# Modulation rows of a two-layer diffusion transformer: two parts first by stationary weights, the other rows in 32-column strips beside other stages

## The chip, the cores and the metric

The kernel runs on one core of one Trainium2 chip. The metric is the device time of one execution in microseconds (us).

## The reference

Two layers (D = 1024) over 256 context tokens and 1024 latent tokens, all in 32-bit floats. In each layer the conditions c and c_ctx give a modulation vector of six parts of 1024 values:

```python
def adaln(cond, w, b):
    mod = jax.nn.silu(cond) @ w + b        # w: (1024, 6144)
    return jnp.split(mod[:, None, :], 6, axis=-1)
...
def modulate(x, shift, scale):
    return x * (1 + scale) + shift
```

Parts 0 and 1 are shift and scale ahead of the token mixer, part 2 the gate on its result, parts 3 and 4 shift and scale ahead of the experts, part 5 the gate on their sum. The token mixer projects the modulated tokens, runs a windowed attention (8 heads) and a latent attention (8 heads, dense), merges the two by sigmoid gates and projects the result. After a layer norm a router chooses for each of 16 experts 128 latent tokens (and in layer 0 also 32 context tokens) by top-k. The experts' SwiGLU results, times part 5, are added into the stream, and a second layer norm ends the layer.

## The kernel before

One instruction stream is written by hand for each engine: TensorE (PE) for all products and transposes, VectorE (DVE) and ScalarE (ACT) for what reads PSUM, GpSimd (POOL) for copies and indirect DMAs, and SyncE (SP) for nearly all loads and stores. A stream waits on counters (`wait_ge`). On SP a DMA is issued when all before it in the stream have been.

The stages of a layer, in order:

1. *Modulation rows of layer 0* (`ada_products(0)`). SP loads w_ada in 12 chunks of 512 columns (2 MB each, `ada_chunk`), and between them the projection weights. For a chunk PE multiplies eight times with the two condition vectors as the stationary side (128x2) and 512 columns of weights moving, and adds the bias with a ninth product of one row (L594). ACT copies the 2x512 result out, POOL stores it to `mod_rows` in DRAM, SP loads all 96 rows of 128 back, PE transposes them, ACT copies them to `modT`, and DVE adds 1 to the scales.
2. *Projections*, one tile of 128 tokens after another (ten tiles). The first waits for all projection weights (`wp_in`).
3. *Attention*, four latent blocks of two tiles, eight head pairs each; layer 0 has a ctx block of eight head pairs before. A head pair n has three parts: A and B (two heads of the latent attention) and W (the window heads). For each part PE computes the scores, DVE finds the maximum, ACT computes the exponentials, PE transposes them in three groups (ci = 0, 1, 2: four, four and two blocks of 128) into PSUM banks 6 and 7 in turn, and ACT or DVE copies each group to `PT` (`copy_chunks`, `copy_chunk`). A bank is free for the next group when its copy is done (`pt_a` counts the copies of ACT, `pt_d` those of DVE, `free_bank` waits).
4. *Merge* (`merge_block`): eight blocks f of 128 output channels, each over three token chunks (256, 512, 512). Per chunk PE multiplies the outputs of both attentions (4 + 4 products) and the gate inputs (8 + 8). SP loads the block's 1.5 MB of weights (`weights`) into one of two buffers, in a loop over pairs of blocks.
5. *Output projection and layer norm* (`y_step`), one tile after another. PE computes 16 products of 512 columns, the router product of two tiles before (`router`, 16 columns), and eight transposes of the tile before; DVE reads y first (`y_used`), then norms.
6. *Choice of tokens*: softmax, transposes of the affinities, top-k on DVE, `select`. In layer 0, PE computes the 12 chunks of layer 1's rows here, eight before `select` and four after it, with the first two chunks loaded during stage 5.
7. *Experts*: 16 experts, weights through a ring of 12 slots of 1 MB. POOL gathers tokens and scatters the results.

`mms` (L575 before, L621 after) and `tr` (L579, L625) issue most products and transposes, so their lines stand for many places. SP's loads all have line L354.

## Time and profile before

| | us |
|---|---|
| median of three runs | 4645.54 (4643.63 to 4647.64) |
| the profiled execution | 4643.44 |
| its span, first to last instruction | 4641.9 |
| PE busy in the span | 4342.7 (94%) |
| DVE, ACT, POOL busy | 1358.6, 1022.7, 211.5 |
| attention of layer 0 with its context block, 457 to 951: PE busy | 473.14 of 494 |
| merge of layer 0, 951 to 1368: PE busy | 412.72 of 417 |
| output tiles of layer 0, 1368 to 1540: PE busy | 164.73 of 172 |
| one head pair in the steady attention (transposes at 804.53, then 818.44) | 13.91 |
| one merge block (SP at 1003.21, then 1054.78) | 51.57 |
| one output tile in the loop (y at 1451.87, then 1469.04) | 17.17 |

The profile is one execution. Its PE products of 32-bit floats stand there as two records each, so a product of 512 columns is two records. "Idle before" a row is the time in which that engine stood still right before it, with the operation that released it. The granted clock is a share of 2.4 GHz: 1.00 or 0.50.

### The profile page before, as it was taken

How to read it: one execution, taken by the hardware profiler on the slowest of the kernel's cores; microseconds unless marked ns; L12 is line 12 of the kernel's file. 1: busy time of each engine (PE TensorE's matmuls, PEld its weight loads, DVE VectorE, ACT ScalarE, POOL GpSimd, SP SyncE). 2: the span in 40 equal slices, each digit the busy share in tenths (PEclk: the TensorE clock that was granted, in tenths of full speed). 3: DMA queues.
4: the chain of work that ended last, by engine and by line, in shares of the span. 5: the costliest groups of instructions: out<-in, count | busy, mean ns of one | idle time of the engine just before them, and what ended most of it. 6: DMA issues, size and time to landing. Idle time of an engine off the chain costs nothing.

```text
span 4641.9 us, 64584 instructions
## 1 busy us (share of the span) xinstructions
PE 4342.7 (94%) x24906; PEld 3015.4 (65%) x24906; DVE 1358.6 (29%) x3311; ACT 1022.7 (22%) x2363; POOL 211.5 (5%) x252
## 2 busy tenths in 40 slices
PE   8998999999999889999999798999999984999995
PEld 1454666655545359999998455666644444999995
DVE  0232655611114711111110444556410145111113
ACT  0222655510002111111110323555400120000001
POOL 0000000000000010000000000000000000000001
PEclk9999999999999999999999899999999996999998
DMA  8112000111223478888877221001112333999994
GB/s 297 57 47 64 19 15 14 35 59 30 67 77 117 163 248 260 263 264 263 250 239 235 96 77 51 15 14 41 37 41 72 120 121 127 312 315 315 309 315 165
DMA packets 577960, 653.08 MB, mean 141 GB/s; under 512 B 36792, under 2 KB 511368, under 8 KB 577808
## 3 DMA queue, kind: packets, MB, share of 16 engines
q1 hardware_dynamic: 562736, 605.71, 40.8%
q0 software_dynamic: 15072, 45.20, 3.9%
q8 instruction: 114, 1.87, 0.2%
q14 instruction: 38, 0.31, 0.0%
HBM read 579.97 MB, written 70.88 MB: 140 GB/s over the span
## 4 chain that ended last, share of the span: by engine, by line
PE 60%; issue 22%; DVE 5%; DMA 1%; ACT 1%; DVEq 0%; POOL 0%; POOLq 0%; SPq 0%; ACTq 0%
PE PS L575 38%; PE PS L865 6%; PE PS L579 5%; PE PS L728 4%; PE PS L794 2%; PE PS L787 1%; PE PS L971 1%; PE PS L706 1%; DVE arena L1534 1%; DVE arena L1536 1%; DVE arena L1229 1%; DVE arena L1540 1%; DVE arena L1383 1%; PE PS L800 0%; PE PS L714 0%
## 5 line engine op out<-in xcount | busy, mean ns | idle before, releaser
L575 PE MATMUL PS<-arena 128*128 128x160 f32 (+6 forms) x14144 | 2947.9, 370 | 31.8 <-DMA arena<-in_b_ada 13.0
L575 PEld LDWEIGHTS PS<-arena 128*128 128x128 f32 (+1 forms) x14144 | 2085.9, 189 | 874.2 <-issue 755.3
L1229 DVE TENSOR_TENSOR arena<-arena,PS 128x160 f32<-128x160 f32 (+3 forms) x336 | 125.1, 382 | 1608.8 <-ACT arena L1209 938.0
L579 PEld LDWEIGHTS PS<-arena 128*128 128x128 f32 (+1 forms) x3078 | 368.9, 142 | 332.2 <-issue 211.6
L579 PE MATMUL PS<-arena 128*128 128x128 f32 (+1 forms) x3078 | 472.0, 280 | 80.1 <-DVE arena L1229 45.7
L728 PE MATMUL PS<-arena 96*128 96x512 f32 (+1 forms) x800 | 363.7, 537 | 33.6 <-DMA arena<-q_window 18.2
L1209 ACT ACTIVATE arena<-PS 128x160 f32<-128x160 f32 (+1 forms) x256 | 74.5, 291 | 1370.3 <-PE PS L575 1370.3
L865 PE MATMUL PS<-arena 128*128 128x512 f32 x576 | 259.5, 605 | 18.2 <-DVE arena L1229 9.9
L1372 DVE TENSOR_REDUCE arena<-PS 128x1 f32<-128x512 f32 (+1 forms) x384 | 229.9, 600 | 117.9 <-PE PS L728 95.7
L1092 ACT ACTIVATE arena<-PS 128x256 f32<-128x256 f32 (+1 forms) x408 | 198.5, 487 | 238.5 <-PE PS L579 234.3
L865 PEld LDWEIGHTS PS<-arena 128*128 128x128 f32 x576 | 108.6, 193 | 149.7 <-issue 125.2
L1229 DVE TENSOR_TENSOR arena<-PS,arena 128x640 f32<-128x640 f32 (+6 forms) x330 | 113.6, 385 | 284.5 <-ACT arena L1100 145.3
L1082 ACT ACTIVATE arena<-PS,arena 128x1280 f32<-128x1280 f32 (+1 forms) x144 | 177.5, 1233 | 83.7 <-DVE arena L1374 67.1
L1229 DVE TENSOR_TENSOR arena<-arena 128x2 f32<-128x2 f32 (+6 forms) x332 | 165.9, 500 | 67.9 <-ACT arena L1145 23.5
L1131 ACT ACTIVATE arena<-PS 128x512 f32<-128x512 f32 (+1 forms) x40 | 22.2, 554 | 703.5 <-PE PS L575 703.5
L1590 DVE SCALAR_TENSOR_TENSOR arena<-PS,arena 128x512 f32<-128x512 f32 x64 | 48.1, 751 | 378.6 <-PE PS L575 378.6
L728 PEld LDWEIGHTS PS<-arena 96*128 96x128 f32 x800 | 123.3, 194 | 50.4 <-issue 44.5
L794 PE MATMUL PS<-arena 128*64 128x128 f32 x2624 | 155.5, 273 | 0.1
L794 PEld LDWEIGHTS PS<-arena 128*64 128x64 f32 x2624 | 145.7, 137 | 0.4 <-ACT arena L1092 0.4
L1400 DVE CUSTOM_DVE_ANT_0 arena<-PS,arena 128x640 f32<-128x640 f32 (+1 forms) x144 | 111.6, 775 | 96.3 <-PE PS L579 70.7
L1383 DVE COPY arena<-PS 128x512 f32<-128x512 f32 x192 | 131.1, 683 | 3.8 <-PE PS L579 3.8
L1074 ACT ACTIVATE arena<-arena 128x640 f32<-128x640 f32 (+1 forms) x144 | 114.2, 793 | 62.0 <-DVE arena L1404 54.9
(151 smaller groups left out, 1791.0 us busy)
## 6 DMA issues: line engine op xcount, KB each, us to landing
arena<-in_w_exp_gate SPq DMA_DIRECT2D x128, 1024.0 KB, 6.9
arena<-in_w_exp_up SPq DMA_DIRECT2D x128, 1024.0 KB, 9.0
arena<-in_w_exp_down SPq DMA_DIRECT2D x128, 1024.0 KB, 7.7
arena<-in_w_ada SPq DMA_DIRECT2D x24, 2048.0 KB
arena<-in_w_in SPq DMA_DIRECT2D x32, 512.0 KB, 5.4
h_transposed<-arena SPq DMA_DIRECT2D x20, 512.0 KB, 4.2
x_mid<-arena SPq DMA_DIRECT2D x18, 512.0 KB, 2.7
moe_sum<-arena SPq DMA_DIRECT2D x18, 512.0 KB, 2.9
```

The lines of the kernel that those rows point to most:

```text
L575: m = pe.matmul(o, lt, rh, start=start and i == 0, stop=stop and i == n - 1)
L579: return pe.transpose(o, i, ident)
L728: pe.matmul(PS[:, b + i, 0:cn], qMt[0:MQ, u, h, :], kT[0:MQ, h, i * 512:i * 512 + cn], start=True, stop=True).then_inc(s["sM"], 1)
L794: pe.matmul(PS[half(g), 6, P:2 * P], V[:, kt, half(2 * c + g)], PT[:, place("AB"[g], n, kt), :], start=kt == 0, stop=kt == nm - 1)
L865: m = pe.matmul(PS[:, h, :], mst[:, k, :], w_o[:, k, h * 512:(h + 1) * 512], start=k == 0, stop=k == KD - 1)
L1074: A(PW[:, g * nk:(g + 1) * nk], PW[:, g * nk:(g + 1) * nk], ACT.Exp, bias=stat[:, st["negW"] + g:st["negW"] + g + 1], accum_out=stat[:, st ...
L1082: A(PM[:, g, 0:nk], flat(b)[:, 0:nk], ACT.Exp, bias=stat[:, st["negM"] + g:st["negM"] + g + 1], accum_out=stat[:, st["sums"] + 2 + g:st["s ...
L1092: A(PT[:, place(part, n, a0):place(part, n, a1), :].rearrange("p a b -> p (a b)"), PS[:, bank(part, ci), 0:(a1 - a0) * P], ACT.Copy).then_ ...
L1229: return dve.tensor_tensor(o, x, y, op)
L1372: dve.tensor_reduce(mxc[:, g, i:i + 1], PS[:, b + i, 0:min(512, TOK - i * 512)], AX.X, ALU.max)
L1383: dve.tensor_copy(PT[:, place(part, n, a0):place(part, n, a1), :].rearrange("p a b -> p (a b)"), PS[:, bank(part, ci), :]).then_inc(s["pt_ ...
L1400: dve.tensor_tensor_reduce(out=PW[:, g * nk:(g + 1) * nk], in0=flat(b)[:, c0:c0 + nk], in1=mask[:, u, m0:m0 + nk], scale=WSCALE, scalar=-3 ...
```

## The change

Four things are done.

**Parts 0 and 1 of layer 0.** The four chunks with their 2048 columns are loaded first, each with a counter of its own. Now the weights are the stationary side (128x128) and the two condition vectors move (128x2), which gives the parts transposed at once: 16 groups of 8 products. The bias comes from a transposed row, and DVE adds both into `modT`. Nothing is stored and reloaded. The projection weights are loaded after the four chunks, the ones of keys and latents first, and are waited for in three lots (`wp_in`, `wq_in`, `wu_in`).

**The other 20 chunks.** The condition vectors are padded with zeros to 32 columns (`silp`). A chunk is computed as four strips: for each k four products of 128 moving columns whose results go to PSUM partitions 0, 32, 64 and 96, then four of the bias. ACT copies 128x128, and SP stores two times four rows. Eight chunks (parts 2 to 5 of layer 0) are computed in the merge of layer 0, one in each block, right after the 4 + 4 attention products of the first token chunk. Of layer 1's, six are computed in the output tiles 4 to 9, one after the router of tile 8, two after the last router, three during the top-k.

**Loads.** SP issues the chunks in the loops in which it loads what these stages need. w_out, which shares its place with the chunks, is loaded after the last one of layer 0.

**Attention.** DVE copies the group ci = 0 of every part, ACT ci = 1 and 2. Before, DVE copied ci = 1 of A and W and ci = 0 of B. In `maxima` DVE's copy stands before the second of three reductions (before: the third).

The diff, cut:

```diff
+            def ada_load(l, c, buf, u):
+
+                cols = ds(c * 512, 512)
+                ld(buf[:, u], a["w_ada"][l].rearrange("(k p) n -> p k n", p=P)[:, :, cols], G[f"ada_in{u}"])
+                ld(adb[0:1, u, :], a["b_ada"][l:l + 1, cols], G[f"ada_in{u}"])
+
+            def ada_store(l, c, u):
+
+                sp.wait_ge(G["rowc"], c + (9 if l else -3))
+                sp.nop(nofuse=True)
+                for v in range(2):
+                    ld(mod_d[l, ds(v * 48 + c * 4, 4), :], adr[v:P:32, u, :], G[f"mod_st{u}"])
 
             for l in range(DEPTH):
...
@@ -492,8 +494,21 @@
                 sp.wait_ge(*s("sM", of(l, 4, 16, 48)))
                 for ci, (c0, cn) in enumerate(CH[l]):
                     ld(hTr[:, :, c0:c0 + cn], hT_d[:, :, c0:c0 + cn], s[f"hT_in{ci}"])
+                    if l == 0 and ci == 0:
+                        sp.wait_ge(*s("ob", 8 * NPAIR[l]))
+                        ada_load(0, 4, adB, 0)
+                if l == 0:
+                    ada_load(0, 5, adB, 1)
                 with sp.Fori(1, 4) as i:
                     weights(i)
+                    if l == 0:
+                        for u in range(2):
+                            sp.wait_ge(G["ada"], i * 2 + u - 1)
+                            sp.nop(nofuse=True)
+                            ada_load(0, i * 2 + u + 4, adB, u)
+                            ada_store(0, i * 2 + u + 2, u)
+                if l == 0:
+                    sp.wait_ge(G["ada"], 8)
                 ld(w_o, a["w_out"][l].rearrange("(k p) n -> p k n", p=P), s["wo_in"])
...
+                        ada_load(1, c, adC, u)
+                    for t in range(TC + 2):
+                        step1(t, t, False)
+                    with sp.Fori(TC + 2, TT - 1) as t:
+                        step1(t, t, False, lambda: next_ada(t - 4, t - 3, 0))
+                        ada_store(1, t - 4, 0)
+                    step1(TT - 1, TT - 1, True, lambda: next_ada(5, 7, 0))
+                    ada_store(1, 5, 0)
+                    next_ada(6, 8, 1)
+                    ada_store(1, 6, 1)
+                    next_ada(7, 9, 0)
+                    ada_store(1, 7, 0)
+                    next_ada(8, 10, 1)
+                    ada_store(1, 8, 1)
+                    next_ada(9, 11, 0)
+                    for c in range(9, 12):
+                        ada_store(1, c, 1 - c % 2)
...
+            def ada_strips(o, w, b):
+
+                for k in range(KD):
+                    for j in range(4):
+                        pe.matmul(o[j * 32:(j + 1) * 32, :], silp[:, k, :], w[:, k, j * P:(j + 1) * P], start=k == 0, stop=False)
+                for j in range(4):
+                    m = pe.matmul(o[j * 32:(j + 1) * 32, :], onesr[0:1, :], b[0:1, j * P:(j + 1) * P], start=False, stop=True)
+                m.then_inc(G["ada"], 1)
 
             for l in range(DEPTH):
...
+                x_transposes(0)
+                if l == 0:
+
+                    pe.wait_ge(G["silc"], 2)
+                    for c in range(4):
+                        pe.wait_ge(G[f"ad{c}"], 16)
+                        for b in range(4):
+                            j = c * 4 + b
+                            m = mms(PS[:, 6, 2 * j:2 * j + 2], [(adA[:, c, k, b * P:(b + 1) * P], silp[:, k, 0:2]) for k in range(KD)])
+                    m.then_inc(G["adA"], 1)
                     pe.wait_ge(G["mod1"], 1)
-                x_transposes(0)
...
-                        elif part == "A":
-                            pe.wait_ge(*s("pt_a", pa_count(l, lp, n, 1)))
                         elif not full:
                             pe.wait_ge(*s("pt_a", pa_count(l, lp, n, 1)))
-                        elif part == "W":
-                            if ci == 0:
-                                pe.wait_ge(*s("pt_d", pd_count(l, lp, n, 1)))
-                            else:
-                                pe.wait_ge(*s("pt_a", pa_count(l, lp, n, ci + 1)))
+                        elif ci == 2:
+                            pe.wait_ge(*s("pt_d", pd_count(l, lp, n, "AWB".index(part) + 1)))
                         else:
-                            if ci == 1:
-                                pe.wait_ge(*s("pt_a", pa_count(l, lp, n, 4)))
-                            else:
-                                pe.wait_ge(*s("pt_d", pd_count(l, lp, n, 2 + ci // 2)))
+                            pe.wait_ge(*s("pt_a", pa_count(l, lp, n, ci + (1 if part == "W" else 3))))
 
                     def some(ci, a0, a1):
...
                             mms(PS[:, b0 + 1, 0:dn], [(mwt[:, u, 20 + k, :], obT[:, k, d0:d0 + dn]) for k in range(4)])
+                        if l == 0 and ci == 0:
+                            pe.wait_ge(G[f"ada_in{u}"], (i + 1) * 32)
+                            ada_strips(PS[:, set_ + 3, 256:384], adB[:, u], adb[:, u])
+                        if l == 0 and ci == 2:
+                            pe.wait_ge(G["rowc"], f + 1)
...
+                def ada_chunk(c, u, nth, b):
+
+                    pe.wait_ge(G[f"ada_in{u}"], 4 * 32 + 32 * nth + 32)
+                    ada_strips(PS[:, b, 0:P], adC[:, u], adb[:, u])
+
...
                 for t in range(TL[l][0], TC + 2):
                     y_step(t)
                 with pe.Fori(TC + 2, TT) as t:
                     y_step(t)
+                    if l == 0:
+                        pe.wait_ge(G["rowc"], t + 4)
+                        ada_chunk(t - 4, 0, t - 4, 5)
                 router(TT - 2)
+                if l == 0:
+                    ada_chunk(6, 1, 0, 6)
                 x1_transposes(TT - 1)
                 router(TT - 1)
+                if l == 0:
+                    pe.wait_ge(G["rowc"], 8 + 6)
+                    ada_chunk(7, 0, 6, 5)
+                    pe.wait_ge(G["rowc"], 8 + 7)
+                    ada_chunk(8, 1, 1, 6)
+                    pe.wait_ge(G["rowc"], 8 + 9)
+                    pe.wait_ge(G["modT_cp"], 1)
...
-                if l + 1 < DEPTH:
+                if l == 0:
                     pe.wait_ge(*s("y_used", NT[l]))
-                    pe.wait_ge(*s("h2d", NT[l]))
-                    ada_products(l + 1, select)
-                else:
-                    select()
+                    ada_chunk(9, 0, 7, 0)
+                    ada_chunk(10, 1, 2, 1)
+                    pe.wait_ge(G["rowc"], 8 + 10)
+                    ada_chunk(11, 0, 8, 0)
+                    pe.wait_ge(G["rowc"], 8 + 12)
+                select()
+                if l == 0:
+                    pe.wait_ge(G["modr_in"], 32 + 16)
+                    pe.matmul(PS[:, 3, 0:96], mrow[0:96, :], ident[0:96, 0:96], start=True, stop=True).then_inc(G["modT"], 1)
...
                     for ci, (a0, a1) in enumerate(chunks(part, full)):
-                        if ci == (0 if part == "B" else 1) and full:
+                        if ci == 0 and full:
                             continue
...
                     for i in range(3):
-                        if i == 2:
+                        if i == 1:
                             between()
                         dve.wait_ge(*s("sM", sM_count(l, lp, n, part, i)))
...
                         return
-                    ci = 0 if part == "B" else 1
+                    ci = 0
                     a0, a1 = chunks(part, True)[ci]
```

In the rows that follow, a wait stands behind the row that has it. First PE at the start of the program, before and after: 128x16 is the transpose of the conditions, 128x128 the transposes of x, 2x512 an old chunk, 128x2 the new products, and 128x512 the first projection.

```order
L583 MATMUL PS<-arena 128x16 [waits cond_in,const_in]
L575 MATMUL PS<-arena 2x512 [waits ada_in0,silc]
L575 MATMUL PS<-arena 2x512 x7
L594 MATMUL PS<-arena 2x512
L575 MATMUL PS<-arena 2x512 [waits ada_in1]
L575 MATMUL PS<-arena 2x512 x7
L594 MATMUL PS<-arena 2x512
```

```order
L625 MATMUL PS<-arena 128x128 [waits x_in]
L625 MATMUL PS<-arena 128x128 x7
L621 MATMUL PS<-arena 128x2 [waits ad0,silc]
L621 MATMUL PS<-arena 128x2 x31
L621 MATMUL PS<-arena 128x2 [waits ad1]
L621 MATMUL PS<-arena 128x2 x31
L621 MATMUL PS<-arena 128x2 [waits ad2]
L621 MATMUL PS<-arena 128x2 x31
L621 MATMUL PS<-arena 128x2 [waits ad3]
L621 MATMUL PS<-arena 128x2 x31
L621 MATMUL PS<-arena 128x512 [waits h_a,h_d,wp_in,mod1]
L621 MATMUL PS<-arena 128x512 x7
```

The first projection stood behind twelve chunks and the reloaded rows; now it stands behind 128 products of two columns, and the transposes of x (128x128) come before these.

Then SP in the loop over pairs of merge blocks. `g` is the wait for the end of an earlier block, ahead of the weights (w_in, w_oa, w_ob) of the pair's second block; before, the loop ends after them.

```order
L354 DMA arena<-in_w_ob 128x4x128
L483 REGISTER_ALU
L354 ISA [waits g]
L354 DMA arena<-in_w_in 128x8x128
L354 ISA
L354 DMA arena<-in_w_in 128x8x128
L354 REGISTER_ALU
L354 DMA arena<-in_w_oa 64x4x128
L354 ISA
L354 DMA arena<-in_w_oa 64x4x128
L354 DMA arena<-in_w_ob 128x4x128
```

```order
L360 ISA
L360 DMA arena<-in_w_oa 64x4x128
L360 DMA arena<-in_w_ob 128x4x128
L360 ISA [waits ada]
L360 DMA arena<-in_w_ada 128x8x512
L360 DMA arena<-in_b_ada 1x512
L360 ISA [waits rowc]
L360 DMA mod_rows<-arena 4x128
L360 ISA
L360 DMA mod_rows<-arena 4x128
L360 ISA [waits ada]
L360 DMA arena<-in_w_ada 128x8x512
```

Behind the same weights stand now the chunk for the first block of the pair, the store of an older row, and the chunk for the second block.

PE in the loop over merge blocks, first block of a pair, before and after (32x128 are the strips):

```order
L833 ISA [waits mrg]
L575 MATMUL PS<-arena 128x256 [waits mw_in0]
L575 MATMUL PS<-arena 128x256 x7
L575 MATMUL PS<-arena 128x256 [waits hT_in0]
L575 MATMUL PS<-arena 128x256 x15
```

```order
L870 ISA [waits mrg]
L621 MATMUL PS<-arena 128x256 [waits mw_in0]
L621 MATMUL PS<-arena 128x256 x7
L882 REGISTER_ALU
L636 MATMUL PS<-arena 32x128 [waits ada_in0]
L636 MATMUL PS<-arena 32x128 x31
L638 MATMUL PS<-arena 32x128 x4
L621 MATMUL PS<-arena 128x256 [waits hT_in0]
```

Between the eight attention products of 256 columns and the gates PE now waits for the chunk (`ada_in0`) and computes its 36 products.

## Rows read from the trace of the kernel before

**Rows 1.** busy time by stage: length, PE, PEld, DVE, ACT, POOL, clock, DMA share, GB/s

```profile
0.00:131.50 131.50, 104.67 (x229) 19.53 (x229) 2.39 (x15) 10.27 (x19) 6.68 (x16) 0.93 0.78 266
...
1540.00:1678.00 138.00, 113.17 (x295) 30.08 (x296) 76.26 (x140) 17.31 (x37) 9.59 (x17) 0.87 0.56 192
```

**Rows 2.** timeline of the prologue: start us, us, engine, line, operation, [idle before <-releaser]

```profile
5.19 0.43 SPq L354 DMA_DIRECT2D arena<-in_w_ada  x1
...
13.41 9.65 PE L575 MATMUL PS<-arena 128*2 128x512 f32 x16 [5.33 <-DMA arena<-in_b_ada]
...
129.18 1.51 ACT L1008 ACTIVATE arena<-PS,arena 128x128 f32<-128x128 f32 x4 [1.71 <-PE PS L579]
...
131.47 21.20 PE L575 MATMUL PS<-arena 128*128 128x512 f32 x48 [1.55 <-DVE arena L1281]
```

**Rows 3.** timeline and stage row of the last router product of layer 0

```profile
1551.67 3.57 PE L575 MATMUL PS<-arena 128*128 128x16 f32 x16 [1.51 <-ACT arena L1159]
...
1551.30:1558.10 6.80, 3.57 (x16) 3.49 (x16) 1.72 (x6) 1.80 (x3) 0.00 (x0) 0.50 0.05 19
```

**Rows 4.** DMA rate from 0 to 135 us in 40 slices

```profile
GB/s 22 12 332 399 387 274 0 135 406 105 376 345 283 374 69 402 314 302 315 182 405 224 377 214 279 399 406 403 397 387 387 361 401 402 281 7 1 15 0 169
```

**Rows 5.** timeline of one head pair of the attention, layer 0

```profile
803.81 0.59 ACT L1092 ACTIVATE arena<-PS 128x512 f32<-128x512 f32 x1
...
804.09 0.60 PE L728 MATMUL PS<-arena 96*128 96x256 f32 x2
...
804.46 0.68 DVE L1383 COPY arena<-PS 128x512 f32<-128x512 f32 x1
804.53 0.38 PE L579 MATMUL PS<-arena 128*128 128x128 f32 x2
804.95 0.38 ACT L1092 ACTIVATE arena<-PS 128x256 f32<-128x256 f32 x1 [0.55 <-PE PS L579]
...
805.20 0.66 PE L579 MATMUL PS<-arena 128*128 128x128 f32 x4 [0.29 <-DVE arena L1383]
```

**Rows 6.** timeline of the context output of one expert

```profile
1783.84 3.66 PE L971 MATMUL PS<-arena 128*32 128x256 f32 x64
```

**Rows 7.** timeline of SP in the merge, and of a w_ada load in the top-k

```profile
1054.78 1.00 SPq L354 DMA_DIRECT2D arena<-in_w_in  x2
...
1057.88 1.26 SPq L354 DMA_DIRECT2D arena<-in_w_ob  x1
...
1569.13 0.40 SPq L354 DMA_DIRECT2D arena<-in_w_ada  x1
...
1577.08 7.03 PE L575 MATMUL PS<-arena 128*2 128x512 f32 x16 [0.22 <-DMA arena<-in_b_ada]
```

**Rows 8.** timeline of the output tiles: the first, and one in the loop

```profile
1368.06 16.83 PE L865 MATMUL PS<-arena 128*128 128x512 f32 x32 [4.12 <-POOL arena L1690]
...
1444.72 7.11 PE L865 MATMUL PS<-arena 128*128 128x512 f32 x16
```

**Rows 9.** timeline of the output tiles: the next tile after its transposes

```profile
1453.24 7.10 PE L865 MATMUL PS<-arena 128*128 128x512 f32 x16 [0.54 <-DVE arena L1229]
```

**Rows 10.** timeline from the last layer norm to the experts, layers 0 and 1

```profile
1549.34 0.34 SPq L354 DMA_DIRECT2D moe_sum<-arena  x1
...
1558.21 1.81 PEld L579 LDWEIGHTS PS<-arena 128*16 128x16 f32 x10 [3.08 <-DVE arena L1229]
...
1634.04 0.89 POOL L1711 DMA_INDIRECT arena<-x_mid,arena  x1 [0.30 <-issue]
...
1675.41 2.27 ACT L1200 ACTIVATE arena<-PS,arena 128x32 f32<-128x32 f32 x8 [0.27 <-PE PS L939]
...
1677.73 22.50 PE L575 MATMUL PS<-arena 128*128 128x160 f32 x152 [2.36 <-ACT arena L1200]
...
3888.43 1.01 POOL L1707 DMA_INDIRECT arena<-x_mid,arena  x1 [103.33 <-DVE arena L1567]
...
3896.69 18.52 PE L575 MATMUL PS<-arena 128*128 128x128 f32 x151 [1.51 <-ACT arena L1195]
```

More of the change, by code:

```diff
@@ L378, in proj_weights @@
-                return parts
-            def ada_chunk(l, i):
-                for u in range(2):
-                    j = l * 12 + i * 2 + u
-                    if not isinstance(j, int) or j >= 2:
-                        sp.wait_ge(G["ada"], j - 1)
-                    cols = ds((i * 2 + u) * 512, 512)
-                    ld(adaw[l][:, u], a["w_ada"][l].rearrange("(k p) n -> p k n", p=P)[:, :, cols], G[f"ada_in{u}"])
-                    ld(adab[l][0:1, u, :], a["b_ada"][l:l + 1, cols], G[f"ada_in{u}"])
@@ L390, in ada_rows @@
[L390 to L400 removed]
+                        parts.append((w_pj[:, :, (2 * j + g) * WD:(2 * j + g + 1) * WD], w[:, :, c0:c0 + WD], "wq_in"))
@@ L506, in ring_load @@
                     ld(ring[:, c], v[:, :, blk * 256:(blk + 1) * 256], s[f"ring{c // 2 if c < 8 else c - 4}"])
+                if l == 0:
+                    for u in range(2):
+                        ada_store(0, 10 + u, u)
+                    sp.wait_ge(G["mod_st0"], 4 * 32)
+                    sp.wait_ge(G["mod_st1"], 4 * 32)
+                    for v in range(2):
+                        ld(mrowB[v * 32:(v + 1) * 32, :], mod_d[0, v * 48 + 16:(v + 1) * 48, :], G["modr_in"])
                 sp.wait_ge(*s("mrg", 8 * NCH[l]))
@@ L520, in _, with step1 @@
                 ld(xr, x_rows(l, TL[l][0]), s["xr_in"])
-                def step1(t, n, last):
+                def step1(t, n, last, between=None):
                     n = t - TL[l][0]
@@ L526, in step1 @@
                         ld(xr, x_rows(l, t + 1), s["xr_in"])
+                    if between:
+                        between()
                     sp.wait_ge(*s("x1", n + 1))
@@ L943, in expert @@
                     first = isinstance(e, int) and e == 0
+                    if l == 0 and first:
+                        pe.wait_ge(G["modT_cp"], 2)
                     pe.wait_ge(*s("xa", e + 1))
@@ L1132, in merge_block @@
                         A(sg[:, set_, 1, 0:cn], PS[:, set_ * 4 + 3, 0:cn], ACT.Sigmoid).then_inc(s["sg"], 1)
+                        if l == 0 and ci == 0:
+                            act.wait_ge(G["ada"], f + 1)
+                            if not isinstance(i, int):
+                                act.wait_ge(G[f"mod_st{u}"], i * 32)
+                            A(adr[:, u, :], PS[:, set_ * 4 + 3, 256:384], ACT.Copy).then_inc(G["rowc"], 1)
                 for u in range(2):
-                    merge_block(u, u)
+                    merge_block(0, u)
                 with act.Fori(1, 4) as i:
                     for u in range(2):
-                        merge_block(i * 2 + u, u)
+                        merge_block(i, u)
                 def ln_a(t):
@@ L1172, in step_a, with ada_rows @@
                     ln_a(t)
+                def ada_rows(c, u, nth, b):
+                    act.wait_ge(G["ada"], 8 + c + 1)
+                    act.wait_ge(G[f"mod_st{u}"], 4 * 32 + 32 * nth)
+                    A(adr[:, u, :], PS[:, b, 0:P], ACT.Copy).then_inc(G["rowc"], 1)
+                if l == 0:
+                    act.wait_ge(G["modT"], 1)
+                    for v in range(2):
+                        m = A(modT[:, 0, v, 2:6, :].rearrange("p a b -> p (a b)"), PS[:, 7, v * 32:(v + 1) * 32], ACT.Copy)
+                    m.then_inc(G["modT_cp"], 1)
+                    act.wait_ge(G["mod1"], 2)
                 for t in range(TL[l][0], TC + 2):
@@ L1310, in _ @@
                 h_half(0)
-                dve.wait_ge(*s("wp_in", 16 * 14))
+                if l == 0:
+                    dve.wait_ge(G["const_in"], 16 * 6)
+                    for i in range(DEPTH):
+                        dve.tensor_scalar(sinks[:, i, 1, :], sinks[:, i, 0, :], -1.0, None, ALU.mult).then_inc(G["bars"], 1)
+                dve.wait_ge(*s("wu_in", 16 * 3))
                 def step(t, n, last):
```

192 lines of the change are left out of this document (90 added, 102 removed).

## The prediction

> **What bounds the kernel now.** I read the busy time by stage first, then the chain of waits, then the order of instructions in time at each place that the diff touches. TensorE (PE) is busy in nearly all of the span, so the question at each place is whether PE waits, and for what. Two stages are not filled by useful PE work [rows 1]. Up to 131.5 us PE does nothing but modulation rows: 104.67 us busy, at 266 GB/s of loads; the first projection starts at 131.47 us [rows 2]. And from the last output tile to the experts (1540 to 1678 us) PE is busy for 113.17 us, but the top-k on DVE and then the last four chunks of layer 1's rows set the end. In the attention PE stands once per head pair, until a copy on DVE frees a bank [rows 5].
>
> **Prologue: parts 0 and 1 by stationary weights.** Removed ahead of the first projection: twelve chunks, the store of the rows and their reload. Added: 128 matmuls of two columns. The first 2 MB chunk took 13.41 - 5.19 = 8.2 us from its issue to the first product [rows 2]; now it is issued some 1.5 us earlier, but 0.5 MB of x stands ahead of it, 1.3 us at the 390 to 400 GB/s of the best slices [rows 4]. So products start at about 12.5. The next chunks land 5.3 us apart (2.1 MB at that rate), so PE is the bound if it runs slowly. The nearest row is the router, eight matmuls with 128x128 stationary and 16 columns: 16 records in 3.57 us [rows 3]. Its cost lies in the stationary load, so I take two columns as no cheaper: 0.214 to 0.223 us per record (the last one's drain out or in), 0.218 x 256 = 56 us. That is a row at 1.2 GHz. I take this level because of the same rows: PE worked on the router without a gap, and the stretch after it still shows the granted clock at 0.50. Products end at 68.5. Two adds, the hand-over and the activations that make h (1.51 us, [rows 2]) take about 2.6 more; the first projection starts at 71.1 instead of 131.47: **-60.4**. The projection weights (12.7 MB up to the first three pieces, 18 MB in all, at 266 to 390 GB/s from about 5 us on: 53 to 73 us) hardly reach into this; bounds of the term: -52 (weights late) and -87 (stream at 2.4 GHz, the first rival).
>
> **Strips.** A strip chunk is 36 matmuls, four side by side. The nearest row is the context output of an expert, four strips of 256 columns: 64 records in 3.66 us [rows 6]. Half the columns and 9/8 of the steps give 3.66 / 2 x 9/8 = 2.06, with the change of tiling about 2.1 us; the products of an old chunk took 7.03 [rows 7]. Lower bound 2.0. If they ran one after another: 72 records at 18.52 / 151 = 0.123 [rows 10], 8.9. The Trainium skill (TensorE: Matmul & The Clock Gate, Part 3) measured 2.38x for three column tiles. Scaled to four tiles that would make 2.8 us a chunk out of the same 8.9, so 14 exposed chunks would cost 10 us more than by the row; the expert's row, whose 64 records lie four abreast, does not agree, and I follow the row.
> Eight chunks lie in the merge, where PE hardly waits (412.7 of 417 us busy, in the table above): 8 x 2.1 = **+17**. Six lie in the output tiles. There PE waits 0.54 to 0.7 us per tile for DVE's first read of y [rows 9], and the chunk stands right in front of that wait: 6 x (2.1 - 0.7) = **+8.4**. The rest lie beside the last layer norm and the top-k.
>
> **Merge: a new wait.** In the loop SP issues the mixer weights of both channel blocks of a pair and only then the w_ada chunk for the first of them. The second block's weights wait for g of the block before, the end of an odd block. So SP gets to the chunk only when PE has already begun the even block that needs it. Before, these issues run from 1054.78 to 1059.1 [rows 7]; the chunk follows at 1059.3, behind 1.5 MB that is still flowing. A chunk with nothing ahead of it took from 1569.13 to 1577.08, 7.9 us [rows 7]; with 1 us for the queue it is there at about 1068. PE began the block at 1054 and needs the chunk after eight matmuls of 256 columns: half of 7.11 for 16 records of 512 [rows 8], 3.6 us, at 1057.6. So PE stands about 10.3 us, for blocks 2, 4 and 6. An idle PE then starts at the lower clock: the first output tile, after 4.12 us idle, took 16.83 us where 2 x 7.11 = 14.2 is the rate [rows 8], 2.6 lost. 3 x (10.3 + 2.6) = **+38.7**; bounds +24 (8 each, all the DMA hidden but the issue) and +50. Block 0 has no wait (10 us of products lie ahead of its chunk), odd blocks neither: theirs is issued a block early. The last chunk's row goes out, comes back and is transposed inside block 7, beside 50 us of matmuls; SP's load of w_out moves behind that chunk, still 40 us early.
>
> **Attention: which engine copies which third.** For part W the second third moves from DVE to ACT. DVE's copy ended at 804.46 + 0.68 = 805.14, and PE started the next transposes at 805.20, though free at 804.75 (two records of 0.11 from 804.53) [rows 5]. The third itself was ready at 804.09. ACT takes a bank 0.20 us after its last transpose (804.75 to 804.95); its copy of the first third (803.81) moves away, so it starts at 804.29, takes 0.59 and ends at 804.88. PE goes on at 804.93 instead of 805.20: 0.27 per head pair, 32 pairs a layer, 64 in all: -17, with a little at the outputs **-18**. Nothing new is queued behind it: ACT's next, the exponentials, waits for a maximum that comes 0.3 us earlier, since DVE's copy now stands before its second reduction and no longer before its third. Bounds 0 and -28 (the whole 0.45).
>
> **Choice of tokens in layer 0.** What goes: from the last gather, 1634.04, PE had waited for chunks and rows until 1677.73 [rows 10]. Layer 1 shows the bare way: gather at 3888.43, first expert product at 3896.69, 8.3 us. With 2 us for the context tokens (L1200, 2.27 us) it would start at 1644.3: -33.4. What comes: chunks 7 and 8 stand between the last router product and the transposes of the affinities. Chunk 8's load is issued after the last stores, about 1.3 us after the one at 1549.34, and lands 8 to 9 us later, at 1559.5; its product, perhaps at the low clock, and the copy end at about 1563, where the transposes began at 1558.21. That is +4.7, 0 to +8. Sum **-28.7**. The early load of the expert weights hides nothing that showed; chunks 9 to 11 lie under the top-k, which covered eight of the old, longer ones.
>
> **Sum.** -60.4 + 17 + 8.4 + 38.7 - 18 - 28.7 = -43. The profiled execution took 4643.4 us (span 4641.9, 1.5 around it), 2.1 below the median 4645.5. 4643.4 - 43 = **4600**.
>
> **The rivals.**
> *The two-column stream runs at 2.4 GHz.* It lasts 28 us instead of 56 and ends near 43, with the weights of the first projection there at about 40: start near 47, 24 us more gained, 4576. For it: PE is never idle there for long. Against it: the clock stayed at 0.50 through the router [rows 3]. The Trainium skill's advice (TensorE: Matmul & The Clock Gate, "Why this matters for your kernels") is to keep the engine busy continuously to get the full clock, and by that rule this rival would win; the router row speaks against it. 8%.
> *The merge has no wait*, because the chunk is there in time: 4561. SP's order of issue excludes it unless I misread which block waits. 5%.
> *The attention gains nothing*, because ACT, now late, takes DVE's place in the wait: 4618. 10%.
> *The strips do not run side by side.* A change that does not do what it says: each matmul waits for the one before in the same bank. 8.9 instead of 2.1 us per chunk on 14 exposed chunks is +95, giving 4695, slower. It decides from 2.1 + 43 / 14 = 5.2 us a chunk on. Against it stands the expert's row, the same form with twice the columns [rows 6]. 3%.
>
> **How the numbers follow.** The forecast as it stands has 74%. Its own range is 4580 to 4620: prologue +8 or -5, merge wait +11 or -15, attention +18 or -10, choice of tokens 5 either way do not all fall on one side. The first and third rival lie within 4574 to 4622, which leaves out the merge without a wait, the serial strips and some of the unnamed: range **4574 to 4622**. About 0.2% (9 us) is what a measurement of this kernel tells from no change. Faster by more than that: 0.94. Within: 0.02. Slower: 0.04, the serial strips and a little for something unseen.
>
> **What would show it.** Right: the first 512-column product at 71 us, the granted clock at 0.5 up to there; three waits of 10 us on in_b_ada or in_w_ada in the merge, each at the start of a block and 103 us apart; strip chunks of 2.1 us; output tiles with a chunk at 18.6 us instead of 17.2; 13.6 instead of 13.9 us per head pair; the first expert product about 15 us after the top-k ends. Wrong: a first projection near 47 us, no waits in the merge, strips of 8 us, or a head pair still at 13.9.

## The result and the profile after

| us | before | after |
| --- | --- | --- |
| median of four runs each | 4645.95 (4643.63 to 4647.64) | 4607.82 (4603.86 to 4610.69) |
| the profiled execution | 4643.44 | 4603.86 |
| its span | 4641.9 | 4602.2 |

The ratio is 0.9918, 95% interval 0.9901 to 0.9935: 38 us faster. The forecast was 4600, range 4574 to 4622. Its sum was made for the profiled executions: -43 us was forecast between the two, and -39.6 is measured.

By stage, the rows of the changed kernel that answer to [rows 1] (stage, its length, then busy time with the number of records on PE, PEld, DVE, ACT and POOL, granted clock, DMA share, GB/s): up to the first projection, the merge, the output tiles, and from the last layer norm to the experts.

```profile
0.00:68.50 68.50, 57.72 (x268) 57.19 (x268) 2.48 (x15) 2.98 (x6) 0.21 (x4) 1.00 0.80 265
881.00:1353.00 472.00, 437.63 (x1731) 237.07 (x1731) 41.20 (x73) 24.98 (x58) 0.72 (x2) 0.97 0.23 74
1353.00:1530.00 177.00, 173.91 (x871) 91.94 (x872) 72.13 (x115) 38.91 (x75) 11.74 (x19) 0.98 0.56 200
1530.00:1645.00 115.00, 39.26 (x594) 32.47 (x593) 78.51 (x144) 13.67 (x36) 3.77 (x5) 0.60 0.59 199
```

The first stage is 68.5 us long where it was 131.5. The merge is 55 us longer than its 417, and PE stands still in it for 34 us. The last stage has 39 us of PE's work instead of 113.

The prologue in time (start us, us, engine, line, operation, [idle before <-releaser]), to be laid beside [rows 2]:

```profile
11.62 54.75 PE L621 MATMUL PS<-arena 128*128 128x2 f32 x256 [3.57 <-DMA arena<-in_w_ada]
...
66.41 0.26 DVE L1315 TENSOR_TENSOR arena<-PS,arena 128x16 f32<-128x16 f32 x2 [61.28 <-PE PS L621]
66.70 1.50 ACT L1064 ACTIVATE arena<-PS,arena 128x128 f32<-128x128 f32 x4 [62.05 <-DVE arena L1315]
...
68.71 2.05 PE L621 MATMUL PS<-arena 128*128 128x512 f32 x2 [2.34 <-DVE arena L1373]
```

256 records take 54.75 us without a gap, 0.213 from start to start, so the loads of w_ada are never waited for after the first. The next 512-column product starts at 68.71.

The merge, PE at the start of three blocks:

```profile
1003.15 3.64 PE L636 MATMUL PS<-arena 128*32 128x128 f32 x64 [10.20 <-DMA arena<-in_b_ada]
1006.73 0.46 PE L638 MATMUL PS<-arena 1*32 1x128 f32 x8
...
1123.35 3.38 PE L636 MATMUL PS<-arena 128*32 128x128 f32 x64 [10.41 <-DMA arena<-in_b_ada]
...
1242.96 3.32 PE L636 MATMUL PS<-arena 128*32 128x128 f32 x64 [10.12 <-DMA arena<-in_b_ada]
```

These are the three waits of the forecast, 120 us apart. SP's queue shows why, at the first of them: the mixer weights of the second block, then the chunk that PE is about to want.

```profile
989.71 1.00 SPq L360 DMA_DIRECT2D arena<-in_w_in  x2
990.89 1.73 SPq L360 DMA_DIRECT2D arena<-in_w_oa  x2
992.71 0.55 SPq L360 DMA_DIRECT2D arena<-in_w_ob  x1
993.51 0.38 SPq L360 DMA_DIRECT2D arena<-in_w_ada  x1
```

A head pair of the attention, where [rows 5] had PE waiting 0.29 us for DVE's copy:

```profile
744.47 0.39 ACT L1157 ACTIVATE arena<-PS 128x256 f32<-128x256 f32 x1 [0.78 <-PE PS L837]
...
750.31 0.60 PE L773 MATMUL PS<-arena 96*128 96x256 f32 x2
750.51 1.04 ACT L1149 ACTIVATE arena<-PS 128x512 f32<-128x512 f32 x2 [0.71 <-PE PS L625]
750.74 1.08 PE L625 MATMUL PS<-arena 128*128 128x128 f32 x6
...
758.13 0.39 ACT L1157 ACTIVATE arena<-PS 128x256 f32<-128x256 f32 x1 [0.78 <-PE PS L837]
```

The two transposes and the four behind them are now one row of six: no wait between them. ACT's copy of the sums (its first and last row here) comes back after 758.13 - 744.47 = 13.66 us; it was 13.91.

The choice of tokens, for [rows 10]:

```profile
1547.61 3.64 PE L636 MATMUL PS<-arena 128*32 128x128 f32 x64
...
1550.26 0.33 DVE L1315 TENSOR_TENSOR arena<-arena 128x160 f32<-128x160 f32 x1
...
1553.53 3.33 PE L636 MATMUL PS<-arena 128*32 128x128 f32 x64 [1.70 <-DMA arena<-in_b_ada]
...
1557.61 1.26 PE L625 MATMUL PS<-arena 128*16 128x128 f32 x10 [0.40 <-ACT arena L1240]
```

DVE has the affinities ready at 1550.6; PE transposes them at 1557.61, behind chunks 7 and 8. Later on the first expert product starts at 1644.53, 5.3 us after the gathered tokens' first transposes at 1639.19, and no chunk is waited for.

### The profile page after: what moved, and what is told of

It is laid out like the page before. It is cut to its first block, busy times and chain, and to the rows that moved or that the text cites. A ratio compares the mean times of both kernels' runs of the same rounds, so it can differ in the third digit from the quotient of the medians.

```text
span 4602.2 us, 66997 instructions
## 1 busy us (share of the span) xinstructions
PE 4258.2 (93%) x26172; PEld 3086.2 (67%) x26172; DVE 1371.3 (30%) x3314; ACT 1019.6 (22%) x2360; POOL 199.0 (4%) x228
## 4 chain that ended last, share of the span: by engine, by line
PE 73%; issue 11%; DVE 4%; DMA 1%; ACT 1%; DVEq 0%; SPq 0%; POOL 0%; POOLq 0%; ACTq 0%
PE PS L621 47%; PE PS L625 6%; PE PS L773 6%; PE PS L907 6%; PE PS L831 3%; PE PS L824 2%; PE PS L751 1%; PE PS L1040 1%; DVE arena L1632 1%; DVE arena L1634 1%; DVE arena L1638 1%; DMA arena<-in_b_ada 1%; DVE arena L1315 1%; PE PS L636 1%; PE PS L837 1%
## 5 line engine op out<-in xcount | busy, mean ns | idle before, releaser
L621 PE MATMUL PS<-arena 128*128 128x128 f32 (+7 forms) x14016 | 2829.2, 363 | 21.4 <-ACT arena L1222 5.0
L621 PEld LDWEIGHTS PS<-arena 128*128 128x128 f32 x14016 | 2108.9, 194 | 722.3 <-issue 613.1
L625 PEld LDWEIGHTS PS<-arena 128*128 128x128 f32 (+1 forms) x3078 | 369.7, 141 | 317.1 <-issue 220.3
L773 PE MATMUL PS<-arena 96*128 96x512 f32 (+1 forms) x800 | 364.0, 537 | 32.1 <-DMA arena<-q_window 17.7
L1315 DVE TENSOR_TENSOR arena<-PS,arena 128x64 f32<-128x64 f32 (+5 forms) x332 | 113.8, 383 | 355.3 <-PE PS L907 147.3
L907 PEld LDWEIGHTS PS<-arena 128*128 128x128 f32 x576 | 109.0, 194 | 142.9 <-issue 126.8
```

The costliest lines, as they stand in the source:

```text
L621: m = pe.matmul(o, lt, rh, start=start and i == 0, stop=stop and i == n - 1)
L625: return pe.transpose(o, i, ident)
L773: pe.matmul(PS[:, b + i, 0:cn], qMt[0:MQ, u, h, :], kT[0:MQ, h, i * 512:i * 512 + cn], start=True, stop=True).then_inc(s["sM"], 1)
L907: m = pe.matmul(PS[:, h, :], mst[:, k, :], w_o[:, k, h * 512:(h + 1) * 512], start=k == 0, stop=k == KD - 1)
L1315: return dve.tensor_tensor(o, x, y, op)
```

## The experiments

Each is the changed kernel with one edit. Times are medians; "gained" is against its 4607.8.

### SP's order in the merge

```diff
-                    weights(i)
-                    if l == 0:
+                    if l:
+                        weights(i)
+                    else:
                         for u in range(2):
+                            weights(i, (u,))
                             sp.wait_ge(G["ada"], i * 2 + u - 1)
```

> The changed kernel, but in the merge SP issues the w_ada chunk of the even block right behind the first block's mixer weights, ahead of the second block's. Theory (the three waits come from SP's order of issue): all three waits of 10.1 to 10.4 us go, and with them about 2.6 us each of work at the lower clock, so the output tiles start 38 us earlier than in the changed kernel and its time falls from 4607.8 to about 4570. Rival 1 (the load is late because 1.5 MB of mixer weights flows beside it): the waits shrink to a few us and 15 to 25 us are gained. Rival 2 (the waits covered something that PE would wait for anyway, as the second block's weights, now later): nothing or under 5 us gained, and a wait on w_in shows in the odd blocks.

Measured: 4571.97 (4567.89 to 4574.72), ratio to the kernel before 0.9839 (0.9825 to 0.9852). 35.8 us gained. PE at the block that had the first wait, and SP's load for it, now 54 us earlier (it was at 993.51 in the changed kernel):

```profile
993.00 1.95 PE L638 MATMUL PS<-arena 128*32 128x128 f32 x64
994.89 0.42 PE L640 MATMUL PS<-arena 1*32 1x128 f32 x8
995.24 20.05 PE L623 MATMUL PS<-arena 128*128 128x256 f32 x62
```

```profile
939.68 0.37 SPq L360 DMA_DIRECT2D arena<-in_w_ada  x1
```

From the last head pair to the output tiles it takes 437.2 us, 472.7 in the changed kernel and 417.8 before. So the waits, with the work at the lower clock behind them, cost 35.5 us, and eight strip chunks 19.4, or 2.4 each. The load wasn't slow; it was asked for late. Neither rival shows.

### The old attention

The edit puts back every line of the diff on which engine copies which third, and `if i == 2` for DVE's place.

> The changed kernel with the attention of the kernel before: DVE copies the second third of parts A and W again and ACT the first, and DVE copies behind the second reduction. Theory of the prediction: a head pair goes back from 13.66 to 13.91 us, as in the two traces, so 64 pairs give back 13 to 16 us (18 by the forecast): about 4622. Rival (the shorter head pair has another cause, as a changed phase of the engines or another clock): a head pair stays at 13.66 and the time at 4608.

Measured: 4623.89 (4619.28 to 4625.9), 16.1 lost. Head pairs take 13.91 again. In the list of PE's waits one line has grown (engine, line, releaser: us in total, times, longest). It is DVE's copy, for which PE waits 2.1 us in 5 times in the changed kernel and 17.7 us in 57 times in the kernel before:

```profile
PE PS L625 <- DVE arena L1487: 18.4, 59, 0.4
```

The 16.3 us by which its sum has grown answer to the 16.1 us lost.

### Parts 0 and 1 by strips too

```diff
-                        for b in range(4):
-                            j = c * 4 + b
-                            m = mms(PS[:, 6, 2 * j:2 * j + 2], [(adA[:, c, k, b * P:(b + 1) * P], silp[:, k, 0:2]) for k in range(KD)])
+                        for k in range(KD):
+                            for j in range(4):
+                                m = pe.matmul(PS[j * 32:(j + 1) * 32, (0, 1, 2, 6)[c], 0:P], silp[:, k, :], adA[:, c, k, j * P:(j + 1) * P], start=k == 0, stop=k == KD - 1)
```

ACT copies each strip block, PE transposes it, and DVE reads columns 32j + v where it read 2j + v.

> The changed kernel with parts 0 and 1 made by strips too, as the later chunks are: 36 us of stationary loads go, each 2 MB chunk takes 2 to 3.9 us when it lands, its rows are copied and transposed. Theory (the stream of 256 stationary loads at the lower clock, 54.75 us, is the bound of the prologue and nothing else is near): the last chunk lands near 28, the activations can begin near 34, and the first projection waits for its weights (3.8 MB behind the chunks at 390 GB/s) until about 38 instead of 68.7: 28 to 30 us gained, about 4579. Rival (the loads are the bound soon after: the weights of the first projection land only near 56, when the loads of the changed kernel end): 12 us gained, about 4596.

Measured: 4580.88 (4572.29 to 4584.45), 26.9 gained.

```profile
11.78 3.64 PE L662 MATMUL PS<-arena 128*32 128x128 f32 x64 [3.53 <-DMA arena<-in_w_ada]
...
29.12 3.19 PE L662 MATMUL PS<-arena 128*32 128x128 f32 x64 [1.99 <-DMA arena<-in_w_ada]
...
38.78 21.80 PE L621 MATMUL PS<-arena 128*128 128x512 f32 x48 [5.62 <-DMA arena<-in_w_in]
```

The first projection starts at 38.78 instead of 68.71 and now waits for its own weights. The stationary stream was the bound, as the theory says; behind it the loads are next, 30 us earlier. Of the 30 us 27 arrive at the attention. In between DVE waits until 57.24 for the small constants, which are loaded last, and PE stands 1.2 us at 61.8 for work of ACT that comes behind it; where the rest goes was not looked into.

### Chunks 7 and 8 behind the affinities

```diff
-                    pe.wait_ge(G["rowc"], 8 + 6)
-                    ada_chunk(7, 0, 6, 5)
...
-                    ada_chunk(8, 1, 1, 6)
...
+                    ada_chunk(7, 0, 6, 0)
+                    ada_chunk(8, 1, 1, 1)
                     pe.wait_ge(G["rowc"], 8 + 8)
```

> The changed kernel with chunks 7 and 8 of layer 1's rows behind the transposes of the affinities instead of ahead of them. Theory (they hold up the choice of tokens, +4.7 in the prediction): the affinities are ready at 1550.6 and transposed from 1557.6 on in the changed kernel, so the top-k and all behind it come 6 to 7 us earlier: about 4601.5. Rival (the chunks then come out behind the top-k, as in the kernel before, and their chain of loads sets the first expert product): under 2 us gained or some us lost.

Measured: 4606.16 (4599.14 to 4610.21). 1.6 us gained, which the medians can't tell from nothing.

```profile
1554.03 2.29 PE L625 MATMUL PS<-arena 128*16 128x128 f32 x10 [3.06 <-DVE arena L1315]
1556.26 3.27 PE L636 MATMUL PS<-arena 128*32 128x128 f32 x64
...
1582.30 3.64 PE L636 MATMUL PS<-arena 128*32 128x128 f32 x64 [5.57 <-DMA arena<-in_b_ada]
...
1624.44 0.58 PE L971 MATMUL PS<-arena 16*128 16x16 f32 x2 [37.96 <-DVEq L1647]
```

The top-k starts 24.4 us after the start of the last record of the output products, where the changed kernel needs 30.3: 5.9 us, just under the 6 to 7 expected. The last chunk is done at 1586.5, 38 us before it could hold anything up. So the two chunks do cost 5.9 us in this stage. That the whole time is shorter by as much is not shown: both kernels' runs spread over more than that (see the last section).

### Strips one after another

```diff
-                for k in range(KD):
-                    for j in range(4):
+                for j in range(4):
+                    for k in range(KD):
```

> The changed kernel, but the 32 matmuls of a strip chunk in the other order: all eight steps of one strip, then of the next. The work is the same. Theory (the four strips run side by side only because neighbours in the stream go to different strips): neighbours now go to the same strip, 64 records of 128 columns take what 64 transposes of 128 columns take, 64 x 0.11 = 7.0 us instead of 1.96; 8 chunks in the merge, 6 in the output tiles and 2 ahead of the affinities stand on the path, 16 x 5.1 = +80 us: about 4690, slower than the kernel before, as the fourth rival had it. Rival (the speed comes from the 32-column weights or from the order of issue not mattering): a chunk stays at 1.96 and the time at 4608.

Measured: 4666.55 (4663.15 to 4670.14), ratio to the kernel before 1.0042 (1.0026 to 1.0057). 58.7 us lost.

```profile
894.11 5.95 PE L636 MATMUL PS<-arena 128*32 128x128 f32 x64
```

The same 64 records take 5.95 us, 0.093 each, against 1.95: a factor of 3.05 from nothing but the order of issue. The expectation had 7.0, hence 80 us instead of 59. The fourth rival was a real danger: with the loops the other way round the whole change is a loss. The Trainium skill (TensorE: Matmul & The Clock Gate, Part 3) says that packed matmuls overlap because each has its own place in the array; this agrees, if neighbours in the stream have different places.

### Wide products in the narrow stream

```diff
                         for b in range(4):
+                            pe.matmul(PS[:, 7, :], ident, adA[:, c, 0, :], start=True, stop=True)
                             j = c * 4 + b
```

> The changed kernel with one more matmul of 512 columns, its result unused, ahead of each of the 16 groups of eight two-column matmuls in the prologue. Theory (the lower clock in the stream comes with its narrow products: only two columns pass in each 0.21 us): the clock rises, a two-column record takes 0.12 to 0.13 instead of 0.214, the stream 256 x 0.125 + 16 x 0.87 = 46 us at most instead of 54.75, and the time falls by 9 us or more in spite of the added work. Rival (two-column records cost 0.21 us at either clock, or the clock stays low for another reason): 14 us more at 2.4 GHz, 28 us more at 1.2.

Measured: 4637.14 (4628.64 to 4640.89), 29.3 us lost: the rival's 28. The first projection starts at 96.00, 27.3 us later than in the changed kernel.

```profile
11.61 2.05 PE L661 MATMUL PS<-arena 128*128 128x512 f32 x2 [3.48 <-DMA arena<-in_w_ada]
13.44 3.41 PE L621 MATMUL PS<-arena 128*128 128x2 f32 x16
...
88.40 2.06 PE L661 MATMUL PS<-arena 128*128 128x512 f32 x2
90.24 3.41 PE L621 MATMUL PS<-arena 128*128 128x2 f32 x16
```

The pattern is the same for 82 us: a period of 5.12 us, 1.84 of it for the two wide records and 3.28 for the 16 narrow ones, which follow each other 0.213 us apart. The profile notes no clock level here before 101.8 us, so the level is read from this distance, which the next experiment shows to be that of 1.2 GHz. PE never stands, and the level stays low. My theory that a few wide products bring the clock up is wrong.

### The clock raised first

```diff
+                    for i in range(12):
+                        pe.matmul(PS[:, 7, :], ident, xb[:, i % 2 * 512:i % 2 * 512 + 512], start=True, stop=True)
                     for c in range(4):
                         pe.wait_ge(G[f"ad{c}"], 16)
```

> The changed kernel with twelve matmuls of 512 columns, their result unused, ahead of the stream of two-column matmuls in the prologue: 24 records of 0.85 us at 1.2 GHz, fewer us if the clock rises on the way, so the stream begins at 22 to 28 instead of 11.6. Theory (the stream doesn't keep the higher clock): two-column records take 0.21 us again after at most a few us, and the first projection comes 8 to 16 us later than at 68.7. Rival (the stream only failed to raise the clock, but keeps it, the first rival of the prediction with its 28 us): records of 0.11 to 0.125 us, the stream takes 28 to 32 us and the first projection comes 5 to 15 us earlier.

Measured: 4612.25 (4610.4 to 4615.92), 4.4 us lost. The stream starts at 18.95. Two stretches of its two-column records alone (length, PE busy with the number of records, granted clock, DMA share, GB/s):

```profile
20.00:23.00 3.00, 3.00 (x30) 1.00 1.05 386
23.10:34.00 10.90, 10.90 (x53) 0.50 1.05 396
```

A stretch also counts the records that only overlap its ends, so the time of one is better taken from start to start: 0.112 us in the first stretch, at 2.4 GHz, and 0.213 in the second, at 1.2. So the narrow record does cost about half at the higher clock, and the stream doesn't hold it: at 23.05 us it falls, with PE busy all the time. The whole first rival would have been 256 x 0.101 = 26 us.

The theory holds, but not its size: the first projection starts at 72.15, 3.4 us later than at 68.71 and not 8 to 16. The 24 wide records took 11.2 us, since the clock rose at 9.4 us, and 4.1 us of the stream ran at the higher level. The Trainium skill (TensorE: Matmul & The Clock Gate, "Why this matters for your kernels") says that keeping TensorE busy brings the full clock. These rows don't agree: here it was busy and the clock fell.

### DVE's place alone put back

```diff
-                        if i == 1:
+                        if i == 2:
                             between()
```

> The changed kernel, but DVE does its copy behind the second reduction of scores instead of the first, as before; which engine copies which third stays as changed. Theory of the prediction (the head pair is shorter because ACT frees the bank of W's second third): still about 13.66 us per head pair. Rival (the earlier place of DVE's copy makes it): 13.9 us per head pair and 13 to 16 us more.

Measured: 4688.11 (4685.9 to 4691.92), 80.3 us lost. Neither expectation. From the list of PE's waits, and two of ACT's copies of the sums:

```profile
PE PS L625 <- DVE arena L1479: 64.8, 126, 1.5
```

```profile
759.75 0.38 ACT L1157 ACTIVATE arena<-PS 128x256 f32<-128x256 f32 x1 [0.78 <-PE PS L837]
...
774.61 0.39 ACT L1157 ACTIVATE arena<-PS 128x256 f32<-128x256 f32 x1 [0.78 <-PE PS L837]
```

A head pair takes 14.86. DVE now copies the first third, whose bank is wanted soonest, but gets to it only behind its second reduction; PE waits 0.51 us for it twice per pair (64.8 us in 126 times).

### The old thirds in DVE's new place

The edit is that of the old attention without the line `if i == 2`.

> The changed kernel with the old choice of which engine copies which third, but DVE's copy stays behind the first reduction: the fourth corner beside 13.91 us per head pair (both old), 13.66 (both new) and 14.86 (new thirds, old place). Theory (the choice of thirds alone frees the bank, and the place only has to fit it: DVE's third must be ready when DVE comes to it): here DVE's third, the second one, isn't ready behind the first reduction, so DVE stands and its maximum comes later: 14.3 to 15.2 us per head pair, 25 to 80 us slower than the changed kernel. Rival (the earlier place alone brings the 0.25 us, whoever copies): 13.66.

Measured: 4620.41 (4618.76 to 4621.74), 12.6 lost, a head pair of mostly 13.87. Again neither. PE waits for the other engine, here in the list and in one pair:

```profile
PE PS L625 <- ACT arena L1157: 16.9, 60, 1.9
```

```profile
469.21 0.59 ACT L1157 ACTIVATE arena<-PS 128x512 f32<-128x512 f32 x1
469.26 0.69 DVE L1487 COPY arena<-PS 128x512 f32<-128x512 f32 x1 [0.76 <-PE PS L625]
...
469.85 0.87 PE L625 MATMUL PS<-arena 128*128 128x128 f32 x6 [0.20 <-ACT arena L1157]
```

DVE does stand before its copy, as the theory has it, but only 0.2 us of that pair reach PE, through ACT's copy.

| us per head pair | DVE copies behind its second reduction | behind its first |
| --- | --- | --- |
| DVE has the second third of A and W | 13.91 | 13.87 |
| DVE has the first third | 14.86 | 13.66 |

Place alone: -0.04. Thirds alone: +0.95. Both: -0.25. The two parts of the change only work together.

### Three edits together

SP's order, parts 0 and 1 by strips, chunks 7 and 8 behind the affinities.

> The changed kernel with three edits together: SP's order in the merge, parts 0 and 1 by strips, chunks 7 and 8 behind the affinities. They lie in different stages, so their gains should add: 36 + 27 + 2 to 6 us less than 4607.8: 4539 to 4543, a better kernel than both. Rival (an earlier prologue moves later loads into each other's way, or chunks wait for stores): 4550 or more.

Measured: **4538.4** (4537.35 to 4543.05), ratio to the kernel before 0.9767 (0.9754 to 0.9781): 69.4 us gained over the changed kernel, 108 over the one before. The single gains add up to 35.8 + 26.9 + 1.6 = 64.3, or 68.6 with the 5.9 that the trace gives the last one; between the profiled executions it is 65.5. The first projection, the transposes of the affinities and the first expert product now start at:

```profile
38.80 21.58 PE L623 MATMUL PS<-arena 128*128 128x512 f32 x48 [5.33 <-DMA arena<-in_w_in]
...
1491.20 2.29 PE L627 MATMUL PS<-arena 128*16 128x128 f32 x10 [3.06 <-DVE arena L1325]
...
1579.54 20.65 PE L623 MATMUL PS<-arena 128*128 128x160 f32 x128 [2.40 <-ACT arena L1296]
```

## Why the prediction was right, point by point

| term, us | forecast | measured between the profiles |
| --- | --- | --- |
| prologue | -60.4 | -62.8 (131.47 to 68.71) |
| merge: chunks and waits | +55.7 | +54.8 |
| attention, both layers | -18 | -13.6 (6.6 and 7.0) |
| output tiles and choice of tokens | -20.3 | -18.1 |
| all the rest | 0 | +0.1 |
| sum | -43 | -39.6 |

**Prologue.** The stream took 54.75 us against 56: the record without its drain, 0.213, is the pace, and products began at 11.62, 0.9 earlier than assumed. The lower clock came as forecast, but its ground was thin, and that part is luck: the router's row lasts 3.57 us and can't tell what a stream of 55 us does, and wide products start at the lower level too (the first projection's records are 0.85 us apart and 0.43 three records later). The announced sign, a granted clock of 0.50, isn't in this profile: no level is noted there until 71.6 us, and the column prints 1.00 for the prologue. The distance of the records tells the level. It is 0.213 all along here; with the clock raised first it was 0.213 at 0.50 and 0.112 at 1.00. The bound of -87 doesn't fit the first rival's own start near 47 us, which makes -84.

**Merge.** Place, number, cause and size of the waits were right: 10.20, 10.41 and 10.12 us against 10.3, and with the work behind them at the lower clock 35.5 in all against 38.7. Strips were a little dearer, 2.4 us a chunk instead of 2.1 (1.95 for the 64 products, 0.42 for the eight of the bias, 0.053 each against 0.030, which I had priced like the others). That the two errors, -3.2 and +2.4, nearly cancel is luck. The spacing of the waits is 120 us, not 103: a pair of blocks grows by its chunks and its wait.

**Attention.** This is the term that missed most: 13.6 instead of 18. A head pair became 0.25 us shorter instead of 0.27 in three of the four blocks, but only 0.15 in the eight pairs of the last one. The third rival, no gain, is excluded by the old attention's +16.1. The wait that I named, PE's for DVE's copy, did go. But the reason I gave was half of it. I put the gain down to ACT freeing the bank, and took DVE's new place for a side effect; the four corners show that the new thirds cost 0.95 us per head pair unless DVE comes to its copy earlier.

**Output tiles and choice of tokens.** Up to the end of the last output product +8.2 against +8.4, but by luck: a tile with a chunk takes 18.83 us instead of 17.17, 1.66 more where I had 1.4, and only five of the six chunks stand ahead of that product. Then -26.3 where the forecast has -28.7. Within it the two chunks ahead of the affinities cost 5.9 where I had 4.7. The first expert product comes 18.4 us after the end of the top-k, not the 15 that I gave as a sign.

**Rivals.** The stream at 2.4 GHz was priced nearly right (26 us by the measured records, 28 forecast) and didn't happen. The merge did wait. The serial strips are 58.7 us dearer, not 95, since a serial chunk costs 4.0 us more, not 6.8; with 5.95 + 0.42 us it still lies beyond the 5.2 from which they decide, and 4666.55 is slower than the kernel before.

## What to carry to other kernels

A chunk that is loaded inside another loop's body is as early as its place in the queue, not as its buffer: move the issue in front of whatever waits for the current block, here worth 36 us, nearly as much as the whole change. When work is shared between two engines in another way, move the place in their programs with it; here one half alone lost 0.95 us per head pair, the other gained 0.04, and both together gained 0.25. Small products with few rows went four abreast only when neighbours in the stream used different strips (1.95 us against 5.95). With 128x128 weights for two columns PE did nothing but load weights, 0.213 us for each record, and at the lower clock.

## What was not expected of the hardware

**The clock under narrow products.** With two-column products PE stayed at 1.2 GHz through 55 us without a gap, and also through 82 us with a 512-column product ahead of each 16 records. Started at 2.4 GHz, it fell to 1.2 after 4.1 us of them.

**Loop turns differ, mostly by the clock.** Between two blocks of eight head pairs, where PE's loop turns, the distance of two of ACT's copies of the sums is 17.01 and 19.23 us in one layer of the changed kernel and 18.35 and 18.42 in the other. Over the eight profiles with the new attention it lies between 16.6 and 19.9, while most pairs within a block repeat to 0.02. PE waits there 2.6 to 3.2 us, with no releaser in the list of waits:

```profile
PE PS L773 <- issue: 11.4, 4, 3.1
```

It is mostly not this wait that makes the difference. The four turns of the changed kernel, from one of ACT's copies to the next (stretch, its length, PE busy and so on as above, the granted clock third from the end):

```profile
544.30:561.31 17.01, 13.86 (x119) 9.74 (x120) 8.57 (x21) 8.11 (x16) 1.49 (x4) 1.00 0.02 4
656.94:676.17 19.23, 16.57 (x119) 11.33 (x120) 8.76 (x21) 8.10 (x17) 1.49 (x4) 0.82 0.02 4
2954.80:2973.15 18.35, 15.40 (x119) 10.76 (x120) 8.67 (x21) 8.07 (x17) 1.49 (x4) 0.91 0.01 3
3068.69:3087.11 18.42, 15.62 (x119) 10.56 (x120) 8.77 (x21) 8.11 (x16) 1.49 (x4) 0.91 0.01 3
```

The same 119 records keep PE busy for 13.86 us at 1.00 and for up to 16.57 where the clock falls behind the wait. The longest turn even has the shortest wait, 2.64 us against 3.09 in the shortest turn. All 32 turns of the eight profiles follow this: nine without a fall take 16.6 to 17.0 us, fifteen with a granted clock near 0.91 take 18.0 to 18.8, and eight near 0.82 take 19.2 to 19.9. What the wait is, and why the clock falls behind it in one turn and not in another, I did not test.

The four turns together take 73.0 us in the changed kernel's profile, and 70.3 to 76.5 in the eight. That is about what the changed kernel's runs spread (4603.86 to 4610.69), though no trace of a longer run is there to show that it is the same. It is why the 5.9 us of the two chunks had to be read from the stage and not from the medians.
